# Gates of 64 of 256 tokens reach the table of experts by scattering transfers instead of one-hot products

## The reference

```
s1, i1 = lax.top_k(s[..., 0, :], PEER_TOPK)
s2, i2 = lax.top_k(s[..., 1, :], PEER_TOPK)
top_s, top_c = lax.top_k(cand, PEER_TOPK)           # cand = s1 + s2, all pairs
idx = i1[top_c // 16] * 128 + i2[top_c % 16]
g = softmax(top_s)                                  # 16 gates of one head
u = take(expert_down, idx);  act = gelu(x . u)
out = sum over the 128 picks of (g * act) * expert_up[idx]
```

## Time and profile before

| what | value |
|---|---|
| median of 3 runs | 2107.09 us (2106.19 to 2109.6) |
| the profiled execution | 2105.34 us, of which the span is 2103.1 us |
| granted TensorE clock | 0.999 of full speed |
| PE busy | 2080.9 us, 99% |
| DVE busy | 1453.8 us, 69% |
| ACT busy | 1274.2 us, 61% |
| POOL busy | 365.7 us, 17% |
| bytes moved by transfers | 373.16 MB, 177 GB/s over the span |

### The profile page before, as it was taken

How to read it: one execution, slowest core, us unless ns; L and a number is a source line. 1 busy time by engine, 2 the same in 40 slices (tenths; PEclk the granted TensorE clock), 3 DMA queues, 4 the chain that set the end, 5 groups by cost and what they waited for, 6 DMA issues and landing times.

```text
span 2103.1 us, 32329 instructions
## 1 busy us (share of the span) xinstructions
PE 2080.9 (99%) x12464; PEld 1807.7 (86%) x12464; DVE 1453.8 (69%) x2582; ACT 1274.2 (61%) x2171; POOL 365.7 (17%) x177
## 2 busy tenths in 40 slices
PE   8999999999999999999999999999999999999998
PEld 8889988888888888887899888888888888788997
DVE  7969988889855555567589888898555555533346
ACT  6654588877644444466645888877544444544564
POOL 1457700000000000012477000000000000154231
PEclk9999999999999999999999999999999999999999
DMA  6455555555566666664456556555666666856344
GB/s 227 151 161 171 180 174 170 166 173 170 162 201 191 198 193 190 197 206 131 141 170 181 174 161 176 169 164 174 191 194 192 195 194 191 269 178 192 107 141 130
DMA packets 105467, 373.16 MB, mean 177 GB/s; under 512 B 12204, under 2 KB 15684, under 8 KB 104932
## 3 DMA queue, kind: packets, MB, share of 16 engines
q1 hardware_dynamic: 105316, 371.11, 58.3%
HBM read 369.97 MB, written 1.10 MB: 176 GB/s over the span
## 4 chain that ended last, share of the span: by engine, by line
PE 95%; DVE 3%; DMA 1%; ACT 1%; issue 0%; POOL 0%; SPq 0%; DVEq 0%; ACTq 0%
PE ps L184 23%; PE ps L178 18%; PE ps L180 17%; PE ps L179 17%; PE ps L185 11%; PE ps L1039 3%; DMA raw<-in_w_qk_dram 1%; PE ps L1018 1%; PE ps L1062 1%; DVE WL L166 1%; PE ps L2143 1%; PE ps L2151 0%; PE ps L2170 0%; DVE arena L754 0%; PE ps L1065 0%
## 5 line engine op out<-in xcount | busy, mean ns | idle before, releaser
L161 ACT ACTIVATE WH<-raw 128x1024 fp32r<-128x1024 f32 x680 | 717.6, 1057 | 483.3 <-PE ps L180 415.7
L166 DVE TENSOR_TENSOR WL<-raw,WH 128x1024 fp32r<-128x1024 f32 x554 | 680.6, 1230 | 70.8 <-ACT WH L161 70.4
L184 PE MATMUL ps<-X,WH 128*128 128x512 f32 x2016 | 716.7, 399 | 3.0 <-DVE WL L166 2.9
L171 POOL TENSOR_TENSOR WL<-raw,WH 128x1024 fp32r<-128x1024 f32 x126 | 314.5, 2500 | 1621.5 <-ACT WH L161 1620.6
L185 PE MATMUL ps<-X,WL 128*128 128x256 f32 x2016 | 563.2, 279 | 0.0
L184 PEld LDWEIGHTS ps<-X,WH 128*128 128x128 f32 x2016 | 379.1, 188 | 90.1 <-DVE WL L166 3.3
L185 PEld LDWEIGHTS ps<-X,WL 128*128 128x128 f32 x2016 | 380.9, 189 | 0.0
L178 PE MATMUL ps<-WH,X 128*128 128x512 f32 (+1 forms) x960 | 377.9, 394 | 2.1 <-DVE X L365 0.9
L180 PE MATMUL ps<-WH,X 128*128 128x512 f32 (+1 forms) x960 | 373.6, 389 | 0.0
L179 PE MATMUL ps<-WL,X 128*128 128x512 f32 (+1 forms) x960 | 373.3, 389 | 0.0
L178 PEld LDWEIGHTS ps<-WH,X 128*128 128x128 f32 x960 | 180.3, 188 | 42.1 <-issue 2.5
(11 more groups left out here) (307 smaller groups left out, 2336.8 us busy)
## 6 DMA issues: line engine op xcount, KB each, us to landing
raw<-in_l_down_dram SPq DMA_DIRECT2D x256, 512.0 KB, 3.7
raw<-in_l_up_dram SPq DMA_DIRECT2D x256, 512.0 KB, 4.2
raw<-in_l_wq_dram SPq DMA_DIRECT2D x32, 512.0 KB, 3.7
raw<-in_w_qk_dram SPq DMA_DIRECT2D x24, 512.0 KB, 3.9
raw<-in_w_gates_dram SPq DMA_DIRECT2D x24, 512.0 KB, 3.6
raw<-in_l_nat_dram SPq DMA_DIRECT2D x16, 512.0 KB, 3.5
raw<-in_l_wout_dram SPq DMA_DIRECT2D x16, 512.0 KB, 3.6
raw<-in_l_win_dram SPq DMA_DIRECT2D x16, 512.0 KB, 4.5
```

The lines of the kernel that those rows point to most:

```text
L161: a.activation(WH[:, i % NW, :], raw[:, i % NW, :], ACT.Copy).then_inc(w_high, 1)
L166: v.tensor_tensor(WL[:, i % NW, :], raw[:, i % NW, :], WH[:, i % NW, :], ALU.subtract).then_inc(w_low_v, 1)
L171: g.tensor_tensor(WL[:, i % NW, :], raw[:, i % NW, :], WH[:, i % NW, :], ALU.subtract).then_inc(w_low_g, 1)
L184: t.matmul(PS[:, bank, :], w[0], X2[:, k, :, :].rearrange("p w t -> p (w t)"), start=first, stop=False)
```

## The change

The gates of tokens 0 to 63 no longer go through one-hot tables and products. GROUPS is 24: `tokens_of(s)` gives group s the tokens 248-8s to 255-8s, so that groups 0 to 23 cover tokens 255 down to 64, and the "open" tokens are now the last k of the 256 and never more than 192. In their place:

- POOL zeroes a tile BLANK of 1024 columns (half of the new tile LATE), and SP writes it 8 times (512 KB each) into a table of 4 MB in device memory for each layer: for layer 0 after chunks 12, 17, ... 47, for layer 1 after chunks P0+148, P0+160, ... P0+232, which are up chunks 4 to 88 of layer 0. The first of the 8 waits for the zeroed tile; for layer 1 POOL zeroes it again after its scatters were issued.
- DVE computes, ahead of the scaled gates, the place of each pick of partitions 0 to 63, (128 i1 + i2) * 64 + token, and its scaled gate (SPOT and SENT, in rows 124 to 127 of G, tokens 0 to 63, which are free until down chunk 125). Its token number comes from two added operations at the kernel's start.
- POOL issues 128 indirect transfers, one for each pick number, each with 64 elements of 4 bytes (one for each token) that the transfer adds to the table. After every 16 it waits until all earlier ones have landed. Its loop of low parts ends before, at step 43.
- POOL then reads the table back in 16 pieces of 256 KB, two buffers, and multiplies each pair of expert rows of G, tokens 0 to 63, by it: 64 operations of 128 by 128 elements. ACT's split of pair p waits for POOL's product p, and DVE's `down_add` of rows 124 and 125 waits until all scatters have landed.
- Some semaphores are merged (tables, positions, relative bias, block 3's tables and pool products), which gives free ones for the new waits.

```diff
+        with nc.sbuf_tensor("LATE", [128, 4, 4, 2, 64], F32) as LATE:
+            pass
+        BLANK = LATE[:, 2:4, :, :, :].rearrange("p s a j t -> p (s a j t)")
+        spread = [nc.dram_tensor(f"gates_by_expert{l}", [128, 8192], F32, kind="Internal") for l in range(2)]
...
+            v.tensor_tensor(PLACE, ident, iota, ALU.mult).then_inc(vec.sem, vec.up())
+            v.wait_ge(vec.sem, vec.n)
+            v.tensor_reduce(SM[:, 120:121], PLACE, AX, ALU.add).then_inc(vec.sem, vec.up())
...
         def mixer0_gpsimd(g):
+            g.memset(BLANK, 0.0).then_inc(blank_up, 1)
...
-        SPREAD, PACE, GROUPS = 25, 3, 32
+        SPREAD, PACE, GROUPS = 25, 3, 24
+        SPOT, SENT = (G[0:64, n:n + 2, 0:64] for n in (124, 126))
+        def pick(w, j):
+            return w[:, j // 64, j % 64:j % 64 + 1]
+        def tokens_of(s):
+            return 248 - 8 * s
...
+        BLANKS = ({12 + 5 * n: n for n in range(8)}, {P0 + 148 + 12 * n: n for n in range(8)})
+        def blank(s, l, i):
+            if i not in BLANKS[l]:
+                return
+            n = BLANKS[l][i]
+            if n == 0:
+                s.wait_ge(blank_up, l + 1)
+            s.dma_start(spread[l][:, 1024 * n:1024 * n + 1024], BLANK).then_inc(blank_out, 16)
...
+            a.wait_ge(late_up, 64 * l + p + 1)
             a.activation(gh, G[:, 2 * p:2 * p + 2, :].rearrange("p e t -> p (e t)"), ACT.Copy).then_inc(g_high, 1)
...
+            v.scalar_tensor_tensor(out=TW[:, 0, :], in0=TK[:, 0, 1, :], scalar=128.0, in1=TK[:, 0, 0, :], op0=ALU.mult,
+                                   op1=ALU.add).then_inc(vec.sem, vec.up())
+            v.tensor_tensor(SENT.rearrange("p a (h k) -> p a h k", k=16),
+                            gt[0:64, 0].rearrange("p (a h) k -> p a h k", a=2),
+                            SM[0:64, 8:16].rearrange("p (a h) -> p a h", a=2).unsqueeze(3).to_broadcast([64, 2, 4, 16]),
+                            ALU.mult).then_inc(vec.sem, vec.up())
+            v.wait_ge(vec.sem, vec.n)
+            v.tensor_scalar(SPOT.bitcast(U32), TW[0:64, 0, :].rearrange("p (a k) -> p a k", a=2), 64.0, SM[0:64, 120:121], ALU.mult, ALU.add).then_inc(tk_up, 1)
...
         def onehots(v, l, s):
+            if s == 0:
+                v.wait_ge(blank_out, 128 * (l + 1))
...
+            if c == 125:
+                v.wait_ge(gate_add, 2048 * l + 2048)
...
         def peer_gpsimd(g, l):
             wq, down, up = bases(l)
-            for c in range(272):
+            for c in range(44):
                 low_g(g, wq + c + 2)
+            g.wait_ge(blank_out, 128 * (l + 1))
+            g.wait_ge(tk_up, 2 * l + 1)
+            everywhere = bass.AP(spread[l], 0, [[1, 128 * 8192], [1, 1]])
+            for j in range(128):
+                if j and j % 16 == 0:
+                    g.wait_ge(gate_add, 2048 * l + 16 * j)
+                g.indirect_dma_start(out=everywhere, out_offset=bass.IndirectOffsetOnAxis(ap=pick(SPOT, j).bitcast(U32), axis=0),
+                                     in_=pick(SENT, j), in_offset=None, compute_op=ALU.add).then_inc(gate_add, 16)
+            g.wait_ge(prod, GROUPS * l + GROUPS)
+            if l == 0:
+                g.memset(BLANK, 0.0).then_inc(blank_up, 1)
+            g.wait_ge(gate_add, 2048 * l + 2048)
+            for q in range(2):
+                load_late(g, l, q)
+            for p in range(64):
+                q, r = divmod(p, 4)
+                late = G[:, 2 * p:2 * p + 2, 0:64]
+                g.wait_ge(act_tail, N_TAIL * l + TAILS[2 * p + 1])
+                g.wait_ge(late_in[q % 2], 16 * (8 * l + q // 2 + 1))
+                g.tensor_tensor(late, late, LATE[:, q % 2, r], ALU.mult).then_inc(late_up, 1)
+                if r == 3 and q + 2 < 16:
+                    g.wait_ge(late_up, 64 * l + p + 1)
+                    load_late(g, l, q + 2)
+            for c in range(270, 272):
+                low_g(g, wq + c + 2)
```

More of the change, by code:

```diff
@@ L142, in build @@
         acc, x_add = sem("acc_done"), sem("x_added")
-        rel_in, rel_out = sem("rel_in"), sem("rel_out")
+        rel_out = sem("rel_out")
         trig_up = sem("trig_up")
+        blank_up, blank_out, gate_add = sem("blank_up"), sem("blank_out"), sem("gates_added")
+        late_in, late_up = [sem(f"late_in{i}") for i in range(2)], sem("late_gated")
         def load(s, i):
@@ L496, in mixer0_sync @@
             s.dma_start(pos_i, d["pos"]).then_inc(pos_in, 16)
-            s.dma_start(AR[0:32, 28160:29184], d["cd"]).then_inc(rel_in, 16)
-            s.dma_start(AR[0:32, 29184:29208], d["rel"]).then_inc(rel_in, 16)
+            s.dma_start(AR[0:32, 28160:29184], d["cd"]).then_inc(pos_in, 16)
+            s.dma_start(AR[0:32, 29184:29208], d["rel"]).then_inc(pos_in, 16)
             for i in range(10, 18):
                 load(s, i)
+                blank(s, 0, i)
             s.wait_ge(rel_up, 1)
@@ L1003, in peer_sync @@
                 load(s, i)
+                blank(s, 0, i)
+                if l == 0:
+                    blank(s, 1, i)
         def load_keys(s, l):
@@ L1164, in rows_scalar @@
         def rows_scalar(a, l, s, js):
-            a.wait_ge(hot, 64 * l + 2 * s + 2)
+            a.wait_ge(hot, 2 * GROUPS * l + 2 * s + 2)
             for j in js:
@@ L1176, in fold_scalar @@
             n = fold_from(c)
-            a.wait_ge(fold_v, 32 * l + s + 1)
-            a.activation(G[:, n:128, 8 * s:8 * s + 8], gate_view()[:, n:128], ACT.Copy).then_inc(fold_a, 1)
+            a.wait_ge(fold_v, GROUPS * l + s + 1)
+            a.activation(G[:, n:128, tokens_of(s):tokens_of(s) + 8], gate_view()[:, n:128], ACT.Copy).then_inc(fold_a, 1)
         def copy_beside(a, l, c):
@@ L1194, in gelus @@
                 a.wait_ge(added, n)
-                a.activation(g[:, :, k:256], g[:, :, k:256], ACT.Gelu_apprx_tanh).then_inc(act_tail, 1)
+                a.activation(g[:, :, 0:256 - k], g[:, :, 0:256 - k], ACT.Gelu_apprx_tanh).then_inc(act_tail, 1)
             if k:
-                o = PS[:, b:b + 2, 0:k]
+                o = PS[:, b:b + 2, 256 - k:256]
                 a.wait_ge(added, n + 1)
@@ L1390, in scale_columns @@
             o = ONE[:, s % 2, 0]
-            v.wait_ge(hot, 64 * l + 2 * s + 2)
+            v.wait_ge(hot, 2 * GROUPS * l + 2 * s + 2)
             v.tensor_tensor(o, o, tokens8(EXP2, s), ALU.mult).then_inc(col_s, 1)
@@ L2090, in build @@
         MXB, SUB = SM[:, 80:96], SM[:, 96:112]
[L2091 to L2093 removed]
+        last_in = sem("skew_and_final_gain_in")
+        ai_a, ai_v, po_mm, po_up = (sem(n) for n in (
+            "ai_by_scalar", "ai_by_vector", "pool_products", "pooled"))
         q2_up, k2_up, v2_a, v2_v = sem("q2_up"), sem("k2_up"), sem("v2_by_scalar"), sem("v2_by_vector")
@@ L2113, in block2_sync @@
             s.wait_ge(b_mm, STEPS)
-            s.dma_start(FG, d["rows"][0:1, RW_FG:RW_FG + 1024].to_broadcast([128, 1024])).then_inc(fg_in, 16)
+            s.dma_start(FG, d["rows"][0:1, RW_FG:RW_FG + 1024].to_broadcast([128, 1024])).then_inc(last_in, 16)
             for i in range(G0 + 19, END):
```

102 lines of the change are left out of this document (51 added, 51 removed).

## The result

The changed kernel takes 2146.48 us (median of 6 runs, 2143.34 to 2150.26) against 2106.49 us of the kernel before: a ratio of 1.019 with a 95% interval of 1.0177 to 1.0203. It is 40 us slower; 17 us faster was forecast. The profiled execution has a span of 2141.5 us against 2103.1, 38.4 us more.

A forecast was written before the change was run, and what follows sets the result against it. TensorE was taken to bound both down stages: 2107.1 us minus 17.1 for 16 groups, everything added costing nothing, gives 2090.0 us. The range was 2086 to 2103 us.

The forecast's parts named there:

- What bounds the kernel: Both down stages: TensorE busy 317.95 of 318 us, so an instruction taken from it is worth its whole time.
- what a group is worth: Down stages: each removed one-hot group saves TensorE 1.07 us, 17.1 us for 16 groups in two layers.
- The added DVE work: Kernel start, before the picks are turned, and end of down stage: small operations hidden in idle time, 0 us.
- the blanks and the reading back: Table zeroing by SP and reading by POOL: taken as 0 us, at most 30 us if every blank shifted TensorE.
- Rival 2: Blanks and reading back crowd weight transfers, up to 30 us reaching TensorE: 2097 to 2120 us; chance 0.11.
- The scatters: POOL beside the down stage: 128 issues at 1.2 us plus 31 us of landings, 185 us, wholly hidden.
- The edge: Before TensorE's first up product: scatters must end by 559 us, giving 304 us from 255.2.
- Rival 1: Late scatters stall TensorE before the first up product; at 2.4 us an issue 2158 us; chance 0.16.
- turning point: POOL's scatters: from 2.20 us an issue on, the change makes the kernel slower instead of faster.
- Rival 3: Down stage: DVE's operations shut POOL out of writing descriptors, some 3600 us; chance 0.02.

The follow-up runs named there:

- the experiment with one tensor read: Changed kernel with DVE's low parts of down chunks 28 to 127 as a product of one tensor with 1.0, output wrong: 2136.09 us (one run).

## Why the prediction was wrong

- **What bounds the kernel, and what a group is worth: right.** PE ends the down stage at 566.3 us as forecast, and without the scatters the kernel takes 2090.25 us where 2090.0 was forecast.
- **The added DVE work, the blanks and the reading back at nothing: right.** They are all in the kernel without scatters, and it loses nothing. Rival 2 (crowded transfers) is out. The queue's row shows 8.47 MB and 3.8% of the engines' time for all that POOL moves.
- **The scatters, and there the step failed.** The prediction took 1.2 us for an issue, "about twice SP's issue", and 185 us in all, where the runs show 328. Of the 143 us missing, 59 are the issue itself (212.9 instead of 154), 29 are a gap of 0.30 us behind each that no row of before has, and 66 are pauses, which were no term of the sum at all; the waits for a landing were 11 us less than taken. The price for an issue was scaled from a plain transfer's on SP. The trace after shows that the kind of transfer matters: POOL's own plain ones, the reading back, take it 0.55 us to issue (592.64), as SP's do, and the indirect ones 1.39 at the least. The trace of before showed no indirect transfer, and between ends of 86 and 354 us the value near the lower one had only its likeness to recommend it.
- **The edge: right.** 559 us was forecast for the latest end of the scatters. Those that end at 547 and 555 us in layer 0 cost nothing, those that end at 565 cost 8 us by the medians, and those that end at 585 cost 56.
- **Rival 1 is what happened,** at its place and by its mechanism: PE released by DVE's low part behind ACT's split behind POOL's product, with DVE in `down_add` of row 125 behind the same landing. It had 0.16 and a price of 2158 us, from a single issue price of 2.4 us. Measured by the prediction's own measure, (328 - 20) / 128 = 2.41 us from issue to issue beside the waits for landings, which is beyond its turning point of 2.20. Its 2158 us came near the measured 2146 by luck: the 2.4 us were POOL's time for a product of 1024 columns, while a scatter's 2.41 are issue, gap and pause. The chance was too small.
- **Rival 3 (port conflict) was right in kind and wrong in size.** The prediction dismissed it by the earlier trace rows: POOL's own operation at 2405 ns median beside a busy DVE. That median doesn't bear it out. In that stretch most of DVE's operations beside POOL's read one SBUF tensor, or one beside PSUM. Where POOL's operation began under one that reads two (line 1309, with 0.80 us left), it took 0.67 us longer than the median, and such a row stood in the trace of before:

```profile
195.33 3.15 DVE L1309 TENSOR_TENSOR arena<-arena 128x768 f32<-128x768 f32 x1
```

```profile
197.68 3.07 POOL L171 TENSOR_TENSOR WL<-raw,WH 128x1024 fp32r<-128x1024 f32 x1
```

The trace after shows the conflict at the start of an issue, 35 us in layer 0, more than the 26 us by which PE was late. The Trainium skill ("SBUF — State Buffer", Who interferes with whom) says that a tensor-tensor operation takes only the read interface while descriptor generation needs the write interface, and marks this as inferred; the same section says that with both inputs in SBUF it contends with GpSimd's reads. The prediction left that out and took POOL's product, which reads SBUF, for agreement. Both fit these traces, at different steps of an issue: the beginning waits for a running difference (2.34 us instead of 1.40), and a difference that begins 0.64 to 1.15 us later holds none of 45 scatters. Its rule for a single-tensor operation that uses both ports agrees with the 50 of 50 that such an operation holds in the experiment with one tensor read (the row of 1.70 us).

- **Not foreseen: what PE's standing still costs afterwards,** 1.9 and 2.4 us at half clock. Together it is a tenth of the loss.

No single part of the 328 us is "the" cause: with 20 us less of each layer's stretch (twice the space) 48 us of time come back, the clock's part among them, and with 10 more nearly all the rest. The pauses (66), the rests of DVE's operations (35) and the gaps (29) are each more than the 26 us that were missing in layer 0. Only less of the pauses, and of the waits for a landing, was seen to bring the time back; with shorter rests alone the pauses grew.

## What to carry to other kernels

When a change hands a chain of small operations to an idle engine, its whole verdict is a deadline: work out the latest end, divide the room by the count, and if the trace has no row for the operation, measure it alone before anything is built on it. A median over a busy neighbour clears a conflict only if the neighbour's operations are of the kind that could conflict. An indirect transfer has prices beside its own duration: a gap behind each, pauses that go by the elements over the descriptor space (here they halved when the space doubled or the elements halved), and the rest of whatever VectorE is running out of two SBUF tensors when it begins. Keep a margin larger than the sum of those, since the other side of the edge costs TensorE the wait and, here, half its clock for the first products, while inside it everything is free.

## What the runs showed of the hardware

- An indirect, adding scatter of 64 elements of 4 bytes takes GpSimd 1.39 us at the least and 1.66 in the mean; 32 elements take 1.30 at the least. The next one begins 0.30 us later.
- With 1024 bytes of descriptor space for each partition 128 such scatters pause 24 times for 2.8 us; with 2048 bytes 13 times for 3.2 us; with 1024 bytes and 32 elements 13 times for 3.0.
- A scatter that begins while VectorE reads two SBUF tensors, or one of 128 x 1024 in 0.69 us, lasts 1.26 us longer than what is left of VectorE's operation. An operation with one tensor in PSUM doesn't hold it up (1.39 to 1.43 us in the changed kernel).
- A VectorE operation that begins 0.64 to 1.15 us after the scatter holds it until its own end if it is the one-tensor product (50 of 50), and not at all if it reads two tensors (0 of 45).
- A plain transfer of 256 KB takes GpSimd 0.55 us to issue.
- The 14336 added elements of both layers with 112 picks cost nothing that shows: 2089.65 us against 2090.25 without any.
- After 26 and 24 us without work TensorE ran its first 9 and 12 products at a granted clock of 0.50; after 4.7 and 3.9 us too, the first 13 stood 0.43 us apart; after 1.1 us the clock was granted at 1.00 over the 10 us around.
